# A decoder step's cache loop on one Trainium2 core: TensorE takes its slots in pairs

## The chip, the cores and the metric

The kernel runs on one core of one Trainium2 chip (trn2), in one launch. The metric is device time in microseconds. The core has five engines that run their own instruction streams and meet at semaphores: TensorE (PE in the profile, its weight loads PEld), VectorE (DVE), ScalarE (ACT), GpSimd (POOL) and SyncE (SP). Transfers between memory and the core are DMAs, issued here by SP and POOL and carried by 16 DMA engines.

## The reference

One inference step of a two-layer decoder. In each layer a prompt of 256 tokens and a group of 8 sequences with 8 new tokens each go through the same weights:

```python
h   = RMSNorm(x) @ W_in
mix = concat[ StickBreakingAttn(q,k,v) | Mamba2-SSD(z,xBC,dt) | MultiScalePool(p) ]
x   = x + mix @ W_out
x   = x + W_down( silu(causal_dwconv3(RMSNorm(x) W_gate)) * RMSNorm(x) W_up )
```

The new tokens of each sequence also attend to 2048 cached positions, that is 16 pages of 128 keys and 128 values, 8 heads of 64 each, found through a page table:

```python
z = einsum('bqhd,bkhd->bhqk', qi, k) * scale + hb
log_keep = where(mask, log_sigmoid(-z), 0.0)
later = cumsum(log_keep, axis=3, reverse=True) - log_keep
w = where(mask, exp(log_sigmoid(z) + later), 0.0)
return einsum('bhqk,bkhd->bqhd', w, v)
```

The weight of a position needs the sum over all later positions, so the pages are taken from the last to the first. All numbers are fp32.

## The kernel before

Each layer has an input projection, a mixing stage with the attention to the cache, an output projection and a gated feed-forward part. The projections take most of the time; each fp32 product there is three matmuls on split planes. The change concerns the mixing stage alone, the **cache loop**.

The loop works on two sequences at a time (a pair) and on chunks of 8 pages, 4 of each of the two sequences. `CHUNKS` is 16 for each layer: 4 pairs by 4 chunks. Every engine runs its own hand-written copy of the loop `for qn in range(CHUNKS + 3)` with 8 slots each; order within an engine is the order of the code, and a wait on a semaphore holds up all that stands behind it. What PE does:

- `key_page(q, k)` (the transposes are line 1382): page k of chunk q has landed in `kring`; four 128x128 transposes put it into PSUM bank 4 (even k) or 5 (odd k). Before that PE waits until the page two earlier has been copied out of that bank: ACT copies the even pages, DVE the odd ones (`key_copy`, lines 941 and 2033) into `kT`.
- `chunk_z(q, bb)` (1394): scores of the four pages of one sequence, four matmuls with 32 columns of the array each. `chunk_z(q, 0)` comes in slot 5 of chunk q, `chunk_z(q, 1)` in slot 1 of the next.
- From the scores ACT and DVE make the weights of the chunk: `chunk_logs` on ACT in slot 2, `chunk_relu` and `chunk_argument` (a scan) on DVE in slots 3 and 5, `chunk_weights` (the exponential, 955) on ACT in slot 6, behind the copy of key page 6.
- `weights_T(q)` (1408): four transposes of the weights at the end of chunk q + 1; ACT copies them into `wz` (`weights_out`, 965).
- `value_page(q, k)` (1426): in chunk q + 2, products of those weights with the values in `vring`, with 32 columns of the array each (in the profile eight matmuls, as every fp32 matmul here has two). The first page of a chunk waits for `wz`.
- `step(s)`: the state-space and pooling work of the layer, cut into small steps by the table `MIX`, one in a slot up to slot 101 (of 152): transposes of states (T, 1528), products with 64 rows (N, 1544), with 16 columns (Y, 1534), in 64 columns of the array (y, 1482) and others. They use PSUM banks 3 and 7 in turn; each is read by DVE or ACT in the same slot of their loops, and PE's a step waits until the step two earlier has been read.

In slot k of chunk qn PE thus runs `key_page(qn, k)`, `value_page(qn - 2, k)`, in some slots a piece of the scores, and then `step`. Chunks 0 and 1 have keys alone, chunks 2 to 15 keys and values, chunks 16 and 17 values alone. In this text a chunk is counted by qn, from its first key page on.

SP issues the loads of key pages into a ring of 8, each when PE has transposed the page 8 before it, with the loads of states between them. POOL issues the loads of value pages (`value_in`), one chunk ahead of their use and each when PE has used the page 8 before it; it also has state work of its own in the slots. After the loop come the first products of the output projection (`out_step`).

Of the kernel before, what the change touches and what calls it, by code (L numbers as in the profile page):

```python
# [79 lines left out]
CHUNKS = 4 * PAIRS  # L80
# [47 lines left out]
def build(nc, a, o):  # L128

    with ExitStack() as ctx:  # L130
# [1003 lines left out]
        def _(pe):  # L1134
            def products(l, base, n, planes, half=8, between=None, ready=None, side=None, swap=0,
# [38 lines left out]
                if n > 1:  # L1174
                    with pe.Fori(1 if between else 0, n) as i:
                        one(i + base)

            DOWN = [down for _, down in B_PART]
            def norm_sum(n):

# [51 lines left out]
            for l in range(DEPTH):  # L1232
# [136 lines left out]
                def new_keys():  # L1369
                    pe.wait_ge(n_w, l + 1)  # L1370
                    for pi in range(PAIRS):
                        mm = pe.transpose(ps[6][0:SAMP, P * pi:P * pi + P], zn[:, SAMP * pi:SAMP * pi + SAMP], ident)
                    mm.then_inc(n_T, 1)

                def key_page(q, k):

                    n = 8 * q + k
                    pe.wait_ge(k_loaded[k], l * (16 * CHUNKS) + 16 * (q + 1))
                    if n >= 2:
                        pe.wait_ge(kT_out[("act", "dve")[n % 2]], l * (CHUNKS * 4) + n // 2)  # L1380
                    for j in range(SBT):
                        mm = pe.transpose(ps[4 + n % 2][:, j * P:(j + 1) * P], kring[:, k, j * P:(j + 1) * P], ident)  # L1382
                    mm.then_inc(k_T, 1)
# [184 lines left out]
                    mm.then_inc(unit_done, 1)  # L1568

                for qn in range(CHUNKS + 3):  # L1570
                    for slot in range(8):
                        if qn < CHUNKS:
                            key_page(qn, slot)
                        if 2 <= qn < CHUNKS + 2:
                            value_page(qn - 2, slot)
                        if slot == 1 and 1 <= qn <= CHUNKS:
                            chunk_z(qn - 1, 1)
                        if slot == 1 and qn == 0:
                            new_scores()
                        if slot == 7 and qn == 0:  # L1580
                            new_keys()
                        if slot == 3 and qn >= 6 and qn % 4 == 2:
                            pair_fold((qn - 6) // 4)
                        if slot == 5 and qn < CHUNKS:
                            chunk_z(qn, 0)
                        step(8 * qn + slot)
                    if qn == CHUNKS:
                        out_step(0, 0)
                    if 1 <= qn <= CHUNKS:
                        weights_T(qn - 1)  # L1590
                    if qn == CHUNKS:
                        out_step(0, 1)
                    if qn == CHUNKS + 1:
                        out_step(1, 0)
# [53 lines left out]
        def _(dve):  # L1648
# [206 lines left out]
            for l in range(DEPTH):  # L1855
# [172 lines left out]
                def key_copy(q, k):  # L2028

                    dve.wait_ge(k_T, l * (CHUNKS * 8) + (8 * q + k + 1))  # L2030
                    if q and k % 4 == 1:
                        dve.wait_ge(q_mm, l * GROUPS + (2 * q + k // 4 - 1))
                    dve.tensor_copy(kT[k // 4][:, :, P * (k % 4):P * (k % 4) + P],
                                    ps[5][:].rearrange("p (j s) -> p j s", j=SBT)).then_inc(kT_out["dve"], 1)
# [172 lines left out]
                for qn in range(CHUNKS + 3):  # L2207
                    for k in range(8):
                        slot = 8 * qn + k
                        for s, at_ in enumerate(((CHUNKS, 1), (CHUNKS, 6), (CHUNKS + 2, 7))):  # L2210
                            if (qn, k) == at_:
                                out_lo(s)
                        if qn < CHUNKS and k % 2:
                            key_copy(qn, k)
                        if slot == 0:
                            prompt_low()
                        if slot == 1:
                            new_arguments()
                        if slot == 4:
                            new_sums()  # L2220
                        if slot == 5:
                            dve.memset(wz[:], 0.0)
                            dve.drain().then_inc(wz_zero, 1)
                        if slot == SLOT["y", 0, 0]:
                            dve.wait_ge(kv_stored, l * 64 + 64)
                        if k == 3 and 1 <= qn <= CHUNKS:
                            chunk_relu(qn - 1)
                        if k == 5 and 1 <= qn <= CHUNKS:
                            chunk_argument(qn - 1)
                        if k == 6 and qn >= 6 and qn % 4 == 2:  # L2230
                            pair_low((qn - 6) // 4)
                        if k == 7 and qn >= 5 and qn % 4 == 1:
                            pair_mask((qn - 5) // 4)
                        if slot - 3 in MIX and MIX[slot - 3][0] == "c":
                            head_weights(*MIX[slot - 3][1:])
                        step(slot)
                        norm_y(slot)
# [182 lines left out]
```

## Time and profile before

| | us |
|---|---|
| median of 3 runs | 3304.39 |
| lowest and highest | 3302.07, 3304.97 |
| span of the profiled execution | 3305.7 |
| cache loop of layer 0, first key page to last value page | about 321 to 606 |
| cache loop of layer 1 | about 1945 to 2232 |

The profile is one execution on the core. In a row of a stretch the busy times are those of PE, PEld, DVE, ACT and POOL, each with its instructions behind it. Busy time of an engine is the union of its instructions; matmuls are pipelined and their ends are modelled, so the distance between starts says more than the busy share. "Idle before" is time in which the engine had nothing running, with what released it. The chain of waits is followed back from the last instruction: at each step to what released it. The granted clock of PE is a share of 2.4 GHz; 0.5 is 1.2 GHz.

### The profile page before, as it was taken

Reading aid. Unit: us, or ns where it says so; the run is one execution under the profiler, and the core shown is the slowest. Engines: PE = TensorE matmul, PEld = TensorE weight load, DVE = VectorE, ACT = ScalarE, POOL = GpSimd, SP = SyncE. Lnnn points to the kernel's source line nnn. Section 1 sums busy time; section 2 is a strip of 40 time slices with the busy share of each in tenths; the row PEclk is TensorE's granted clock in tenths of the full one; section 3 lists DMA queues with packets and bytes.
Section 4 is the critical chain, followed back from the end, with each engine's and each line's share of the span. In section 5 each row is a group of like instructions: output and inputs, shape, how many; then the busy total and the mean of one; then the engine's idle time right before and its main releaser. Section 6 shows DMA issues by size and latency. Waiting matters only on the chain.

```text
span 3305.7 us, 62396 instructions
## 1 busy us (share of the span) xinstructions
PE 3213.3 (97%) x23776; PEld 3026.9 (92%) x23776; DVE 1898.2 (57%) x3339; ACT 1346.9 (41%) x1663; POOL 409.6 (12%) x513
## 2 busy tenths in 40 slices
PE   7999998999999999999999999989999999999998
PEld 7999665899999999999999976659999999999998
DVE  4574655466653665466746656454666546654664
ACT  4553665444433333233335546563444333333332
POOL 0000654220000000000200035531100000000002
PEclk9999999999999999999999999989999999999999
DMA  6433799744444444444544448985444444444443
GB/s 188 141 124 104 242 311 300 216 144 153 152 142 153 151 144 152 145 154 138 157 141 128 129 140 273 314 275 164 147 153 148 146 153 148 145 154 143 149 149 101
DMA packets 469101, 554.42 MB, mean 168 GB/s; under 512 B 20635, under 2 KB 414444, under 8 KB 468788
## 3 DMA queue, kind: packets, MB, share of 16 engines
q1 hardware_dynamic: 440275, 466.93, 44.3%
q0 software_dynamic: 26192, 84.73, 7.9%
q8 instruction: 117, 1.92, 0.2%
q10 hardware_dynamic: 2449, 0.27, 0.1%
q14 instruction: 68, 0.56, 0.1%
HBM read 535.50 MB, written 16.38 MB: 167 GB/s over the span
## 4 chain that ended last, share of the span: by engine, by line
PE 92%; ACT 2%; DVE 1%; issue 1%; DMA 1%; PEld 1%; ACTq 0%; DVEq 0%; PEldq 0%; POOLq 0%; POOL 0%; SPq 0%
PE ps L1157 26%; PE ps L1159 26%; PE ps L1158 26%; PE ps L1382 3%; PE ps L1426 2%; PE ps L1394 1%; PE ps L1544 1%; PE ps L1534 1%; PE ps L1471 1%; PE ps L1528 1%; DMA raw<-in_w_out 0%; PE ps L1408 0%; DMA vring<-in_cache_v 0%; ACT wz L965 0%; ACT kT L941 0%
## 5 line engine op out<-in xcount | busy, mean ns | idle before, releaser
L1654 DVE TENSOR_TENSOR wl<-raw,wh 128x1024 fp32r<-128x1024 f32 (+1 forms) x736 | 904.3, 1238 | 994.4 <-ACT wh L776 986.6
L776 ACT ACTIVATE wh<-raw 128x1024 fp32r<-128x1024 f32 (+1 forms) x736 | 764.8, 1041 | 1603.6 <-PE ps L1159 1592.7
L1157 PE MATMUL ps<-fh,wh 128*128 128x320 f32 x2816 | 870.6, 309 | 0.0
L1159 PE MATMUL ps<-fh,wl 128*128 128x320 f32 x2816 | 870.1, 309 | 0.0
L1158 PE MATMUL ps<-fl,wh 128*128 128x320 f32 x2816 | 870.1, 309 | 0.0
L1157 PEld LDWEIGHTS ps<-fh,wh 128*128 128x128 f32 x2816 | 528.5, 188 | 0.2
L1158 PEld LDWEIGHTS ps<-fl,wh 128*128 128x128 f32 x2816 | 528.5, 188 | 0.2
L1159 PEld LDWEIGHTS ps<-fh,wl 128*128 128x128 f32 x2816 | 528.5, 188 | 0.0
L1157 PE MATMUL ps<-hh,wh 128*128 128x320 f32 x1376 | 428.4, 311 | 5.6 <-DVE wl L1654 4.6
L1157 PE MATMUL ps<-ah,wh 128*128 128x320 f32 x1376 | 427.2, 310 | 0.0
L1159 PE MATMUL ps<-hh,wl 128*128 128x320 f32 x1376 | 426.1, 310 | 0.0
L1159 PE MATMUL ps<-ah,wl 128*128 128x320 f32 x1376 | 425.2, 309 | 0.0
L1158 PE MATMUL ps<-hl,wh 128*128 128x320 f32 x1328 | 411.3, 310 | 0.0
L1158 PE MATMUL ps<-al,wh 128*128 128x320 f32 x1328 | 410.3, 309 | 0.0
L1157 PEld LDWEIGHTS ps<-hh,wh 128*128 128x128 f32 x1376 | 259.2, 188 | 7.7 <-issue 5.1
L1157 PEld LDWEIGHTS ps<-ah,wh 128*128 128x128 f32 x1376 | 258.3, 188 | 1.7 <-issue 0.3
L1159 PEld LDWEIGHTS ps<-hh,wl 128*128 128x128 f32 x1376 | 259.1, 188 | 0.0
L1159 PEld LDWEIGHTS ps<-ah,wl 128*128 128x128 f32 x1376 | 258.3, 188 | 0.0
L1158 PEld LDWEIGHTS ps<-hl,wh 128*128 128x128 f32 x1328 | 250.2, 188 | 0.0
L1158 PEld LDWEIGHTS ps<-al,wh 128*128 128x128 f32 x1328 | 249.3, 188 | 0.0
L752 POOL DMA_DIRECT2D out_new_ffn_conv_prompt<-ftail x6 | 3.1, 523 | 1612.1 <-DVE ftail L1746 1612.1
L1382 PE MATMUL ps<-con,kring 128*128 128x128 f32 x1024 | 168.7, 289 | 7.6 <-ACT kT L941 6.9
(405 smaller groups left out, 3683.1 us busy)
## 6 DMA issues: line engine op xcount, KB each, us to landing
raw<-in_w_gate SPq DMA_DIRECT2D x88, 1024.0 KB, 5.1
raw<-in_w_up SPq DMA_DIRECT2D x88, 1024.0 KB, 5.0
raw<-in_w_in SPq DMA_DIRECT2D x72, 1024.0 KB, 5.2
kring<-in_cache_k SPq DMA_DIRECT2D x256, 256.0 KB, 4.2
vring<-in_cache_v POOLq DMA_DIRECT2D x256, 256.0 KB, 4.6
raw<-in_w_down SPq DMA_DIRECT2D x64, 1024.0 KB, 5.4
raw<-in_w_out SPq DMA_DIRECT2D x32, 1024.0 KB, 6.5
raw<-in_w_down SPq DMA_DIRECT2D x32, 768.0 KB, 4.6
```

Of the source, the lines that this page charges most:

```text
L776: act.activation(wh[:, s % 2, half, :], raw[:, s, half, :], ACT.Copy).then_inc(hi_done, 1)
L1157: pe.matmul(out, wh[:, s % 2, kk, w], hi(row), start=first, stop=False)
L1158: pe.matmul(out, wh[:, s % 2, kk, w], lo(row), start=False, stop=False)
L1159: mm = pe.matmul(out, wl[:, s % 2, kk, w], hi(row), start=False, stop=last)
L1382: mm = pe.transpose(ps[4 + n % 2][:, j * P:(j + 1) * P], kring[:, k, j * P:(j + 1) * P], ident)
L1394: mm = pe.matmul(ps[q % 2][32 * j:32 * j + 32, :], qp[:, q // 4, bb, j, :], kT[bb][:, j, :], start=(bb == 0), stop=(bb == 1))
L1426: mm = pe.matmul(ps[6][32 * j:32 * j + 32, 0:P], wz[:, k // 4, k % 4, j, :], vring[:, k, j * P:(j + 1) * P], start=False, stop=last)
L1471: mm = pe.matmul(bank[:, i * T:(i + 1) * T], tk[0:T, 1, h:h + 1].broadcast_to([T, P]), le, start=True, stop=True)
L1528: mm = pe.transpose(bank[:, j * P:(j + 1) * P], s_seq[i % 4][:, 4 * h + j, :], ident)
L1534: mm = pe.matmul(bank[:, j * 16:(j + 1) * 16].rearrange("p (e t) -> p e t", e=2), sT[:, i % 2, j * P:(j + 1) * P], csS[:, 2 * j:2 * j + 2, ...
L1544: mm = pe.matmul(bank[:, j * NS:(j + 1) * NS], xw[0:SAMP, (4 * h + j) * P:(4 * h + j + 1) * P], bm[:, i % 2, h * NS:(h + 1) * NS], start=T ...
L1654: dve.tensor_tensor(wl[:, s % 2, half, :], raw[:, s, half, :], wh[:, s % 2, half, :].bitcast(F32), ALU.subtract).then_inc(lo_done, 1)
```

## The change

On PE two slots are taken together: key pages k and k + 1, the step of slot k, value pages k and k + 1, the pieces of the scores and the like that stood in either slot, and the step of slot k + 1. On DVE the copy of the odd key page moves from its own slot to the head of the even slot before it. Nothing else is touched; the work is the same.

```diff
--- before.py
+++ after.py
@@ -1568,22 +1568,25 @@
                     mm.then_inc(unit_done, 1)
 
                 for qn in range(CHUNKS + 3):
-                    for slot in range(8):
+                    for slot in range(0, 8, 2):
                         if qn < CHUNKS:
                             key_page(qn, slot)
+                            key_page(qn, slot + 1)
+                        step(8 * qn + slot)
                         if 2 <= qn < CHUNKS + 2:
                             value_page(qn - 2, slot)
-                        if slot == 1 and 1 <= qn <= CHUNKS:
+                            value_page(qn - 2, slot + 1)
+                        if slot == 0 and 1 <= qn <= CHUNKS:
                             chunk_z(qn - 1, 1)
-                        if slot == 1 and qn == 0:
+                        if slot == 0 and qn == 0:
                             new_scores()
-                        if slot == 7 and qn == 0:
+                        if slot == 6 and qn == 0:
                             new_keys()
-                        if slot == 3 and qn >= 6 and qn % 4 == 2:
+                        if slot == 2 and qn >= 6 and qn % 4 == 2:
                             pair_fold((qn - 6) // 4)
-                        if slot == 5 and qn < CHUNKS:
+                        if slot == 4 and qn < CHUNKS:
                             chunk_z(qn, 0)
-                        step(8 * qn + slot)
+                        step(8 * qn + slot + 1)
                     if qn == CHUNKS:
                         out_step(0, 0)
                     if 1 <= qn <= CHUNKS:
@@ -2210,8 +2213,8 @@
                         for s, at_ in enumerate(((CHUNKS, 1), (CHUNKS, 6), (CHUNKS + 2, 7))):
                             if (qn, k) == at_:
                                 out_lo(s)
-                        if qn < CHUNKS and k % 2:
-                            key_copy(qn, k)
+                        if qn < CHUNKS and k % 2 == 0:
+                            key_copy(qn, k + 1)
                         if slot == 0:
                             prompt_low()
                         if slot == 1:
```

## Rows read from the trace of the kernel before

**Rows 1.** The page, part 1: busy us, share of the span, instructions.

```profile
PE 3213.3 (97%) x23776; PEld 3026.9 (92%) x23776; DVE 1898.2 (57%) x3339; ACT 1346.9 (41%) x1663; POOL 409.6 (12%) x513
```

**Rows 2.** Stretches, layer 0: us, busy by engine, clock, DMA share, GB/s.

```profile
420.00:480.00 60.00, 57.06 (x616) 39.83 (x617) 29.89 (x58) 35.57 (x72) 29.28 (x41) 1.00 0.96 315
...
540.00:595.00 55.00, 42.74 (x474) 24.14 (x475) 32.25 (x49) 38.90 (x61) 17.93 (x33) 0.91 0.89 291
```

**Rows 3.** PE timeline, chunk 7: start, us, line, operation, count, idle before.

```profile
441.11 0.60 PE L1382 MATMUL ps<-con,kring 128*128 128x128 f32 x4
442.02 0.43 PE L1426 MATMUL ps<-vring,wz 128*32 128x128 f32 x8 [0.31 <-ACT wz L965]
...
444.55 0.66 PE L1528 MATMUL ps<-con,s_seq 128*128 128x128 f32 x4
445.05 0.60 PE L1382 MATMUL ps<-con,kring 128*128 128x128 f32 x4
445.57 0.43 PE L1426 MATMUL ps<-vring,wz 128*32 128x128 f32 x8
445.93 0.66 PE L1382 MATMUL ps<-con,kring 128*128 128x128 f32 x4
446.52 0.43 PE L1426 MATMUL ps<-vring,wz 128*32 128x128 f32 x8
```

**Rows 4.** The same timeline, chunk 16: two value pages in a row.

```profile
588.36 0.65 PE L1426 MATMUL ps<-vring,wz 128*32 128x128 f32 x16 [0.75 <-ACT wz L965]
```

**Rows 5.** Timeline of PE's weight loads at the place of rows 3.

```profile
444.94 0.47 PEld L1382 LDWEIGHTS ps<-con,kring 128*128 128x128 f32 x4
```

**Rows 6.** Waits of PE, chunks 2 to 12, layer 0: us, times, longest.

```profile
PE ps L1426 <- ACT wz L965: 3.1, 8, 0.9
PE ps L1408 <- ACT wq L955: 3.0, 3, 1.3
PE ps L1471 <- DVE pool_lo L2133: 1.0, 1, 1.0
PE ps L1423 <- ACT wz L965: 0.7, 2, 0.4
```

**Rows 7.** The same for layer 1.

```profile
PE ps L1426 <- ACT wz L965: 2.2, 7, 0.4
PE ps L1471 <- DVE pool_lo L2133: 1.9, 1, 1.9
PE ps L1408 <- ACT wq L955: 1.2, 3, 0.4
```

**Rows 8.** Timeline of ACT at the end of chunk 6.

```profile
438.02 0.60 ACT L941 ACTIVATE kT<-ps 128x512 f32<-128x512 f32 x1 [1.85 <-PE ps L1382]
...
439.93 0.63 ACT L955 ACTIVATE wq<-wq 128x512 f32<-128x512 f32 x1
```

**Rows 9.** Chain of waits, layer 0, chunk 15: start, us, what.

```profile
574.78 0.42 PE ps L1426 x8
575.20 0.97 PE ps L1382 x4
576.17 0.59 PE ps L1426 x8
```

**Rows 10.** Stretches as in rows 2: the 10 us that moved most.

```profile
460.00:470.00 10.00, 10.00 (x112) 7.11 (x105) 4.62 (x8) 6.92 (x12) 6.03 (x8) 1.00 1.05 374
```

**Rows 11.** The same, chunks 7 and 12, layers 0 and 1 of each.

```profile
441.10:457.30 16.20, 14.56 (x162) 9.90 (x161) 7.47 (x13) 8.35 (x13) 7.84 (x11) 1.00 0.92 288
2061.40:2081.20 19.80, 19.07 (x163) 12.50 (x162) 7.65 (x13) 8.35 (x13) 7.67 (x11) 0.74 0.93 291
527.10:544.50 17.40, 15.76 (x167) 11.04 (x165) 9.84 (x17) 8.51 (x13) 8.84 (x13) 1.00 0.84 283
2150.90:2173.40 22.50, 21.78 (x166) 14.79 (x165) 10.15 (x17) 8.46 (x13) 8.79 (x12) 0.70 0.78 238
```

## The prediction

> **What bounds the kernel now.** I read the page first. TensorE (PE) is busy for 97% of the span [rows 1], so time is won where PE runs, provided PE is what the stage waits for. The change touches only the cache loop, twice some 300 us out of 3305.7. So I cut that loop into stretches: in the middle of it PE is busy for 57.06 of 60 us, at a granted clock of 1.00, VectorE (DVE) and ScalarE (ACT) for a half and somewhat more; towards the end PE falls to 42.74 of 55 [rows 2]. The middle hangs on PE, the end on something else.
>
> Busy is not work, though, so next I read PE's timeline for the distance from one start to the next. A key page is four full-array transposes, a value page eight matmuls that each use 32 columns of the array. From [rows 3]: four transposes (here T, a state step) that come after 32-column work and before full-array work take 0.50 us to the next start (444.55 to 445.05). A key page between full-array work and a value page takes 0.52 (445.05 to 445.57). A key page between two value pages takes 0.59 (445.93 to 446.52). So coming in from the narrow shape costs 0.07 and going out to it 0.09, and a key page with full-array work on both sides is 0.59 - 0.07 - 0.09 = 0.43. A value page between key pages takes 0.36 (445.57 to 445.93); two value pages in a row last 0.65 against 0.43 for one [rows 4, 3], so a value page followed by another takes 0.22. Going back to the wide shape thus costs 0.36 - 0.22 = 0.14 there and 0.07 in the page that follows. Of the stretch K V K V, 1.90 us, a part is nothing but changes of shape. That is the first thing that the change can move.
>
> The second is in the waits. At each chunk's first value page PE stands idle for the weights that ACT has to copy out after W (0.31 at 442.02 [rows 3]); over chunks 2 to 12 that is 3.1 + 0.7 us in layer 0 and 2.2 + 0.7 in layer 1, 19 waits [rows 6, 7] (the row of line 1423 reads the same in both layers and stands once). W itself, the weights' transpose, waits for ACT's exponential 3 times in each layer, 3.0 and 1.2 us. The only other wait in these stretches is one step's for DVE, 1.0 and 1.9; there is none for a load [rows 6, 7].
>
> **The change part by part.**
>
> *Fewer changes of shape.* No instruction is added or taken away. Two slots K V S, K V S become K K S, V V S. Without steps, K V K V is 2 x (0.59 + 0.36) = 1.90; K K V V is 0.50 + 0.52 + 0.22 + 0.36 = 1.60. Gain 0.30. With a full-array step S in the first slot: before, K 0.52, V 0.36, S 0.50, K 0.52, V 0.36 = 2.26; after, K 0.43, K 0.43, S 0.52, V 0.22, V 0.36 = 1.96 (S taken as four transposes). Again 0.30. A step of another shape (64 rows or 64 columns) has a change on both sides in either order, so two changes of five still go. Key and value pages meet in chunks 2 to 15; steps end at slot 101, in chunk 12. For chunks 2 to 12, where PE is the bound, that is 11 chunks x 4 pairs x 2 layers = 88 pairs: **26.4 us**. Chunks 0 and 1 have no value pages, 16 and 17 no keys and no steps, so nothing changes shape less often there: zero.
>
> *The wait for the weights.* After W, before: one key page, then the value page. After: two key pages and a step first, at least 0.43 us more. The missing time is 0.91 - 0.52 = 0.39 (441.11 to 442.02 against a page that does not wait [rows 3]). It is covered even where there is no step. The idle time of 3.8 + 2.9 = 6.7 us does not count the 0.07 by which an unhindered value page starts before the key page's modelled end (445.05 + 0.60 against 445.57), 19 times 1.3: **8.0 us**. The cover is the second key page; if that waits itself (for DVE's copy), at most these 8 us stay.
>
> *The end of the loop, chunks 13 to 15.* There the chain of waits goes value page 0.42, key page 0.97, value page 0.59, scores [rows 9], partly at half clock, and then through ACT. With the key page moved under the wait for the weights the stretch becomes two value pages, 0.65 [rows 4]: 0.42 + 0.97 + 0.59 - 0.65 = 1.3 saved at best; at full clock, 0.36 + 0.59 + 0.22 - 0.44 = 0.7, less 0.1 for the two key pages after W. Two chunks in each layer show this, and in one of them the loads that GpSimd (POOL) issues may come last: 0 to 5 us, taken **3**.
>
> *What is given back.* W needs ACT's exponential, which follows the copy of key page 6: from the copy's start to the exponential's end 439.93 + 0.63 - 438.02 = 2.54 us [rows 8]. The exponential hangs on PE's page 6, and the pair 6/7 is now 0.30 shorter. Where W waits already (6 chunks, [rows 6, 7]) the 0.30 of that pair is lost, 1.8; in all 22 chunks it would be 6.6. I take **-3**, since most chunks have no such wait.
>
> *Moved work costed at nothing.* DVE copies the odd key page before the step of the even slot, no longer after it: half of DVE's time is free there [rows 2], and the copy is wanted only when the key page two later comes. If it delayed the even steps, PE would wait up to a copy, some 0.6 us (what ACT's takes [rows 8]), less the second slot. SP issues the odd key load a little sooner. POOL waits for "value page used": the even one comes a key page and a step later, the odd one about when it did; value pages are loaded a whole chunk ahead, and in the middle PE never waits for one [rows 6, 7]. What is queued behind POOL's wait is its state work, which has several slots to spare. Nothing to either side of the loop changes; it starts earlier.
>
> Sum: 26.4 + 8.0 + 3 - 3 = 34.4. The profiled span of 3305.7 stands 1.3 above the median of 3304.4; I subtract from the median and give 1 us for steps whose inputs now are late, as two are already (1.0 and 1.9 [rows 6, 7]): **3271 us**, -1.0%. Own range 3259 to 3283: low if the two half-clock stretches of layer 1 go too (below, 8.7) and the end gives its 5; high if all the weights' wait stays and W loses everywhere (8 + 3.6).
>
> The page "TensorE: Matmul & The Clock Gate" of the Trainium skill, Part 3, speaks against this: loading weights overlaps running matmuls only when the row group differs; key pages all use every row. The trace disagrees: key page weights begin loading at 444.94 [rows 5] while T, on all 128 rows, runs from 444.55 for 0.66 [rows 3]. By that rule the sum would be the 3295 of the second rival, by the rows it is 3271.
>
> **The rivals.**
>
> *Transfers pace the middle.* The 16 DMA engines are busy at a share of 0.96 at 315 GB/s there [rows 2]; the same pages in less time need some 9% more (a chunk of some 17 us loses 4 x 0.30 + 8.0/22 = 1.56). If nothing more passes in the busier two thirds, 14 of the 22 chunks, then 14/22 of 31.4 = 20 are lost: 3291. The same time comes out if ACT's chain sets every chunk's length. Against it: one stretch of 10 us moved 374 GB/s at 1.05 [rows 10], and PE has no wait for a page in chunks 2 to 12 [rows 6, 7]. Chance 0.17, for 3283 to 3298.
>
> *The full array doesn't overlap.* If two key pages side by side cost as much as two apart, the 26.4 are gone: 3304.4 - 8 - 3 + 2 = 3295. [Rows 3 and 5] are against it: 0.04. The rule of the Trainium skill above would give this.
>
> *Slower, by the clock.* In layer 1 chunk 7 took 19.80 against 16.20 in layer 0 at the same work, chunk 12 22.50 against 17.40, at a mean granted clock of 0.74 and 0.70 [rows 11]: stretches at 1.2 GHz instead of 2.4, costing 3.6 and 5.1. Longer runs of transposes and more pressed waits at W could bring such stretches into other chunks, at 4.35 each. From eight more on (8 x 4.35 = 35) the gain is gone; in 12 more of the 22 chunks, 3271 + 52 = 3323. For it: two of 22 have it already. Against it: PE has less idle time than before, and layer 0 has none in these two. Slower by over 0.2%: 0.05; five to nine more, and so no change that shows: 0.07.
>
> **How the numbers follow.** Forecast 0.67 (3259 to 3283), transfers 0.17, no overlap 0.04, clock 0.07 and 0.05. What a measurement can tell from no change is about 0.2%, 6.6 us. Faster by more than that (under 3297.8): 0.67 + 0.17 + 0.03 = 0.87; same 0.08; slower 0.05. For 8 in 10 the range takes the forecast's own and most of the transfers': 3258 to 3292.
>
> **What would show it.** Right: PE's timeline has value pages in sixteens of some 0.65 us and key pages in eights; a key page after a key page starts 0.50 or less behind it; no idle time of PE before a value page put down to ACT's weights; waits of W for ACT grown from 4.2 us to 6 to 10; each layer's loop shorter by some 17 us, all other stages as long as before. Wrong: waits of PE for key or value loads and a DMA share above 1 in the middle (transfers); key pages 0.59 apart (no overlap); chunks at a mean clock near 0.7 in both layers (clock); or waits at the steps, where a step that comes sooner finds DVE or ACT not done.

## The result, and the profile after

The changed kernel takes **3274.01 us** (median; 3269.99 to 3287.52), the kernel before 3303.23 (3297.14 to 3304.97) beside it. The ratio is 0.9932, with a 95% interval of 0.9912 to 0.9953: 22 us faster by the ratio, 29 by the medians. The forecast was 3271 in a range of 3258 to 3292, a gain of 33 us. The time lies in the range, the direction and the mechanism are as forecast, and about a third of the gain is missing by the ratio (4 of the 33 us by the medians). Most of what follows is about that third.

The page of the changed kernel, first line and part 1, to set beside [rows 1]. The profiled execution is the slowest of the changed kernel's, some 13 us above their median, so its losses are a little larger than usual:

```profile
span 3285.7 us, 62396 instructions
...
PE 3180.7 (97%) x23776; PEld 3038.2 (92%) x23776; DVE 1912.0 (58%) x3339; ACT 1346.4 (41%) x1663; POOL 410.4 (12%) x513
```

PE does the same 23776 matmuls in 32.6 us less busy time; the span is only 20.0 us shorter. The time at half clock is 97.5 us in both executions, so it does not explain the difference: PE's own work shrank by about what was forecast, and waiting grew. The stretches tell where. First those of the kernel before that were not shown (start and end in us, length, busy time and instructions of PE, PEld, DVE, ACT and POOL, granted clock, DMA share, GB/s): chunks 2 to 12 of layers 0 and 1, chunks 13 to 15 of both, and chunk 8 of layer 0.

```profile
357.60:544.50 186.90, 179.00 (x1899) 124.23 (x1897) 103.26 (x190) 111.67 (x201) 103.53 (x137) 0.99 0.89 293
1976.80:2173.40 196.60, 190.51 (x1897) 131.75 (x1896) 104.36 (x189) 111.80 (x201) 105.88 (x140) 0.93 0.86 281
544.50:588.40 43.90, 33.55 (x364) 17.93 (x365) 25.55 (x40) 29.93 (x51) 13.34 (x25) 0.92 0.89 289
2173.40:2215.60 42.20, 32.76 (x360) 18.15 (x358) 25.54 (x40) 30.02 (x51) 13.44 (x25) 0.92 0.88 289
457.30:473.10 15.80, 15.49 (x166) 10.96 (x165) 6.95 (x11) 9.92 (x16) 8.82 (x12) 1.00 1.06 373
```

The same stretches of the changed kernel, then chunk 8 of layers 0 and 1, and chunks 7 and 12 of layer 0 for [rows 11]:

```profile
357.50:542.60 185.10, 173.23 (x1898) 132.41 (x1897) 111.93 (x191) 111.78 (x201) 104.18 (x136) 0.95 0.89 297
1971.00:2157.20 186.20, 175.47 (x1899) 134.05 (x1898) 109.55 (x189) 111.71 (x201) 106.93 (x141) 0.94 0.89 295
542.60:583.80 41.20, 29.55 (x360) 19.47 (x358) 25.66 (x40) 29.66 (x50) 13.22 (x25) 0.92 0.91 302
2157.20:2198.50 41.30, 29.52 (x360) 19.46 (x357) 25.66 (x40) 29.79 (x50) 13.43 (x25) 0.92 0.90 302
452.60:473.90 21.30, 17.81 (x166) 13.59 (x165) 7.02 (x11) 10.14 (x16) 7.51 (x11) 0.84 0.97 321
2065.10:2088.10 23.00, 19.18 (x166) 14.80 (x165) 7.05 (x11) 10.14 (x16) 7.55 (x11) 0.78 0.90 294
437.60:452.60 15.00, 13.38 (x162) 10.26 (x161) 7.47 (x13) 8.35 (x13) 7.61 (x11) 1.00 0.95 301
523.40:542.60 19.20, 17.58 (x166) 13.39 (x164) 9.90 (x17) 8.49 (x13) 9.12 (x13) 0.82 0.85 300
```

Chunk 7 is what the forecast had in mind: 15.00 us for 16.20 at the same work and full clock. Chunk 8 is the opposite: 21.30 and 23.00 for 15.80. Chunks 2 to 12 together gain 1.8 + 10.4 = 12.2 us where 26.4 + 8 - 3 - 1 = 30.4 were forecast. An average gain of 1.43 in chunk 8 would have brought it to 14.4, so chunk 8 alone loses 6.9 + 8.6 = 15.5 of the missing 18.2. The remaining 2.7 are the difference of larger parts. Chunks 2 to 4 of both layers gain 3.3 us where six times 1.43 = 8.6 were forecast. Chunk 12 of both layers and chunk 7 of layer 1 gain 6.1 where 4.3 were forecast, since half-clock stretches stand there in one execution and not in the other: [rows 11] has them in chunks 7 and 12 of layer 1, the changed kernel in chunk 12 of both layers. The end of the loop, chunks 13 to 15, gains 2.7 + 0.9 = 3.6 for the 3 forecast. The other 4.2 of the 20.0 lie outside these stretches, where nothing was forecast; they are less than the 7.8 us between the lowest and the highest time of the kernel before.

PE's timeline of chunk 8 in layer 0, the analogue of [rows 3], shows both the gain and the loss:

```profile
452.15 0.66 PE L1408 MATMUL ps<-con,wq 128*128 128x128 f32 x4 [1.62 <-ACT wq L955]
452.65 1.04 PE L1382 MATMUL ps<-con,kring 128*128 128x128 f32 x8
453.61 0.64 PE L1426 MATMUL ps<-vring,wz 128*32 128x128 f32 x16
454.07 1.04 PE L1394 MATMUL ps<-kT,qp 128*32 128x512 f32 x8
...
456.94 0.64 PE L1426 MATMUL ps<-vring,wz 128*32 128x128 f32 x16
457.52 0.66 PE L1528 MATMUL ps<-con,s_seq 128*128 128x128 f32 x4
461.31 0.66 PE L1382 MATMUL ps<-con,kring 128*128 128x128 f32 x4 [3.13 <-DMA kring<-in_cache_k]
462.32 0.66 PE L1382 MATMUL ps<-con,kring 128*128 128x128 f32 x4 [0.36 <-DMA kring<-in_cache_k]
462.82 3.14 PE L1534 MATMUL ps<-csS,sT 128*128 128x16 f32 x16
```

Two key pages with a value page behind them take 453.61 - 452.65 = 0.96 from the first start to that of the value page. With 0.52 for the page ahead of the value page [rows 3], the first of the two costs 0.44; 0.43 was forecast for a key page with full-array work on both sides. Two value pages take 0.46 to the next narrow work (453.61 to 454.07) and 0.58 to the next wide work (456.94 to 457.52), as 0.22 + 0.36 says. There is no idle time ahead of the value page at 453.61, where chunk 7 before had a wait of 0.31 for the weights [rows 3]. In exchange W waits 1.62 for the exponential, and then, at 458.18, PE stands still for 3.13 us for a key page. After that the clock row of the trace falls to 0.5 for 6.8 us (from 463.1), and the sixteen matmuls of Y take 3.14.

PE's waits in chunks 2 to 12 of layer 0, to set beside [rows 6] (us in total, times, longest):

```profile
PE ps L1408 <- ACT wq L955: 3.8, 4, 1.6
PE ps L1382 <- DMA kring<-in_cache_k: 3.5, 2, 3.1
PE ps L1471 <- DVE pool_lo L2136: 2.1, 1, 2.1
PE ps L1426 <- ACT wz L965: 0.8, 1, 0.8
```

and of layer 1, beside [rows 7]:

```profile
PE ps L1408 <- ACT wq L955: 4.0, 5, 1.6
PE ps L1382 <- DMA kring<-in_cache_k: 3.8, 2, 3.4
```

The value pages' wait is gone (the 0.8 is the first value page of chunk 13, at 544.44), W waits 7.8 us where it waited 4.2, and a row that before had none heads the new ones: key pages that wait for their load.

At the end of the loop the chain of waits of layer 0 in chunk 15, [rows 9] before, now reads (start, us, what):

```profile
578.74 0.49 ACT kT L941
...
579.38 1.06 PE ps L1382 x8
580.44 0.62 PE ps L1426 x16
...
583.47 5.44 DMA vring<-in_cache_v
```

The value page between the two key pages is out of the chain, as worked out; the copies of keys on ACT stand in it, and a load that POOL issues comes last of all, as was held possible.

### The profile page after: what moved, and what is told of

It is laid out like the page before. It is cut to its first block, busy times and chain, and to the rows that moved or that the text cites. A ratio compares the mean times of both kernels' runs of the same rounds, so it can differ in the third digit from the quotient of the medians.

```text
span 3285.7 us, 62396 instructions
## 1 busy us (share of the span) xinstructions
PE 3180.7 (97%) x23776; PEld 3038.2 (92%) x23776; DVE 1912.0 (58%) x3339; ACT 1346.4 (41%) x1663; POOL 410.4 (12%) x513
## 3 DMA queue, kind: packets, MB, share of 16 engines
q1 hardware_dynamic: 440275, 466.93, 44.3%
## 4 chain that ended last, share of the span: by engine, by line
PE 90%; DVE 2%; ACT 2%; DMA 2%; issue 1%; PEld 1%; DVEq 0%; ACTq 0%; SPq 0%; PEldq 0%; POOLq 0%; POOL 0%
PE ps L1157 26%; PE ps L1159 26%; PE ps L1158 26%; PE ps L1382 3%; PE ps L1394 1%; PE ps L1426 1%; PE ps L1544 1%; PE ps L1534 1%; DMA kring<-in_cache_k 1%; DMA vring<-in_cache_v 1%; PE ps L1471 1%; DMA raw<-in_w_out 0%; PE ps L1408 0%; ACT kT L941 0%; ACT L955 0%
## 5 line engine op out<-in xcount | busy, mean ns | idle before, releaser
L604 POOL DMA_DIRECT2D vring<-in_cache_v x256 | 139.4, 545 | 237.8 <-issue 131.4
```

Source lines behind the costliest of these rows:

```text
L604: pool.dma_start(vring[:, k, :], a["cache_v"][l, page].rearrange("s h d -> s (h d)")).then_inc(v_loaded[k], 16)
```

## The experiments

All ratios are to the kernel before, run beside the kernel in question on the same chip, with 95% intervals. The length of a chunk is the distance between its first key page and the next chunk's in the profiled execution. "The change" is the changed kernel above.

### The change once more

The changed kernel without any edit, to see what of the above returns.

> The changed kernel unchanged, beside the variants on one chip. Theory 1 (two late key pages in chunk 8 give back part of the gain): the times scatter between 3268 and 3288 us, and a profile shows PE waiting for key loads in chunk 8, 2 to 4 us in a layer, with a half-clock stretch behind it. Theory 2 (transfers pace the whole middle): 3274 us, with waits for loads in several chunks. Theory 3 (the clock alone): half-clock stretches without a wait ahead of them.

Measured: 3277.27 us (3271.86 to 3291.24), ratio 0.9937 (0.9915 to 0.9959). The profile is of an execution at the median, span 3274.8 us. Chunk 8 takes 21.8 and 20.0 us, and key pages wait for their loads again, 5.0 us in 4 places (7.3 us in 4 places of the whole run above). That is what the first theory expected.

So the loss in chunk 8 belongs to the kernel and not to one execution. Chunk 12, at half clock in both layers above, is so only in layer 0 here (19.3 us); in layer 1 it takes 16.1. That stretch comes and goes, and no step of the argument should rest on it.

### One part alone: fewer changes of shape

K V V K S S instead of K K S V V S: the value pages are in pairs, so that there are fewer changes of shape, but no second key page and no step stands between W and the first value page.

```diff
                         if qn < CHUNKS:
                             key_page(qn, slot)
-                            key_page(qn, slot + 1)
-                        step(8 * qn + slot)
                         if 2 <= qn < CHUNKS + 2:
                             value_page(qn - 2, slot)
                             value_page(qn - 2, slot + 1)
...
+                        if qn < CHUNKS:
+                            key_page(qn, slot + 1)
+                        step(8 * qn + slot)
                         step(8 * qn + slot + 1)
```

> Fewer changes of shape without the cover for the weights: per two slots PE runs key page, value page, value page, key page, step, step. Two changes of shape in each pair as in the changed kernel, but the first value page of a chunk stands one key page behind the weights' transpose, as before. Theory 1 (26 us from the shape, 8 from the cover): 3280 to 3286 us, the idle time before value pages put down to ACT's weights is back at 5 to 7 us. Rival (the cover brings most): 3292 to 3298 us.

Measured: 3283.72 us (3279.7 to 3286.53), ratio 0.9950 (0.9932 to 0.9968), 16.5 us. In the chunks that nothing else disturbs the gain is what four pairs at 0.30 should give, and a little less: chunks 8, 9, 10 and 11 of layer 0 take 14.7, 16.6, 17.2 and 17.1 us for 15.8, 17.6, 18.1 and 18.3, that is 1.1, 1.0, 0.9 and 1.2 for 1.2. Chunks 5 and 7 gain 0.7 and 0.8; chunk 6 gains nothing, as its wait for the weights grows from 0.31 to 0.92 and a step waits 0.41. Over chunks 2 to 12 of both layers the wait for the weights is 10.3 us, where 5 to 7 were expected and 6.7 stood before. Chunk 4 pays: 20.9 us for 18.4 in layer 0, at full clock, and 22.6 for 17.9 in layer 1. There two steps stand side by side, and the second finds its input not done. PE's timeline of chunk 4:

```profile
391.99 1.16 PE L1503 MATMUL ps<-xtok,xw 128*128 128x128 f32 x8
394.87 0.45 PE L1482 MATMUL ps<-seg,xtok 128*64 128x128 f32 x4 [1.72 <-ACT cs L1012]
```

The price of a change of shape is confirmed where PE has nothing to wait for. The 26.4 us of the sum lie above the interval (10.6 to 22.4): the steps' inputs set the pace in chunk 4, and the weights come later in relation to a faster PE.

### The other part alone: a cover for the weights' wait

From the kernel before: K S V in each slot. The changes of shape are as many as before (where the step is full-array work), but a step stands between W and the first value page, in the chunks that have a step in slot 0 (chunk 8 has none).

```diff
                         if qn < CHUNKS:
                             key_page(qn, slot)
+                        step(8 * qn + slot)
                         if 2 <= qn < CHUNKS + 2:
                             value_page(qn - 2, slot)
...
-                        step(8 * qn + slot)
```

> The cover alone: as before one slot at a time, but the step runs between the key page and the value page (key page, step, value page), so four changes of shape in two slots as before, while the first value page of a chunk now has a step and not only a key page between it and the weights' transpose. Theory 1: 5 to 9 us faster than before, 3292 to 3297; the idle time before value pages put down to ACT's weights falls from some 11 to under 4 us. Rival (the order of steps against pages is what helps, not the shape): 15 us or more faster.

Measured: 3290.68 us (3283.22 to 3298.3), ratio 0.9983 (0.9971 to 0.9996), 5.6 us. The wait of value pages for weights falls from 10.0 us in 21 places of the whole run to

```profile
PE ps L1426 <- ACT wz L965: 5.2, 8, 1.2
```

of which 0.6 lie in chunks 2 to 12, in chunk 8 of the two layers (5.3 before [rows 6, 7]). Chunks 5, 9, 10 and 11 take 14.8, 17.0, 17.6 and 17.6 us for 15.2, 17.6, 18.1 and 18.3: 0.4 to 0.7 each, which is the 0.39 of the prediction and a little more. The 8 us of the sum lie inside the interval's 1.3 to 9.6 us. Shape alone and cover alone add up to 22 us, the change to 21 to 22. That the two agree is a coincidence and does not show that the parts simply add: shape alone loses in chunk 4, where the change does not, and the change loses in chunk 8, where neither part alone waits for a load (14.7 us there with shape alone, 15.7 and, partly at half clock, 17.3 with the cover).

### The copy on VectorE back in its own slot

The order of PE is the change's; DVE copies the odd key page in its own slot again.

```diff
-                        if qn < CHUNKS and k % 2 == 0:
-                            key_copy(qn, k + 1)
+                        if qn < CHUNKS and k % 2:
+                            key_copy(qn, k)
```

> The changed order on PE, but DVE copies the odd key page in its own slot, behind the even slot's step, as before. Theory 1 (the move on DVE costs and brings little): within 4 us of the changed kernel, 3271 to 3281. Rival (the early copy delays the even steps in chunks 4 and 13, where nothing was won): 4 us or more faster, chunk 13 back to 15 us. The other side (the early copy is needed, as the next odd key page waits for it): slower, with waits of PE for DVE's copies.

Measured: 3277.48 us (3268.5 to 3287.97), ratio 0.9942 (0.9920 to 0.9965), no different from the change. PE now waits for DVE's copies, 13.3 us in the whole run instead of 1.9:

```profile
PE ps L1382 <- DVE kT L2036: 13.3, 12, 2.4
```

The waits for key loads in chunk 8 are there as in the change, 5.4 us. Chunk 13 falls from 15.8 to 15.3 us in both layers, chunks 0 and 3 of layer 1 rise by 1.2 (partly at half clock) and 0.6. So the moved copy is worth its place in some chunks and costs in others, and on balance nothing that can be measured. The place where it costs is read in the change's trace, ACT and DVE in chunk 13: DVE takes the copy at 546.17 ahead of the product that ACT waits for, ACT's copy of a key page stands behind that wait, and PE behind the copies.

```profile
546.17 0.69 DVE L2036 COPY kT<-ps 128x512 f32<-128x512 f32 x1
546.78 1.00 DVE L2191 SCALAR_TENSOR_TENSOR y<-y,par,rstd 128x320 f32<-128x320 f32 x2
...
547.36 0.47 ACT L1029 ACTIVATE y_hi<-y 128x320 fp32r<-128x320 f32 x1 [2.48 <-DVE y L2191]
547.73 0.58 ACT L941 ACTIVATE kT<-ps 128x512 f32<-128x512 f32 x1
```

### The loads of three states spread out

Ahead of chunk 8, in slot 59 (chunk 7), SP issues the loads of three states, 512 KB each, one right after the other, and only then the next key loads. Here they are issued in slots 59, 61 and 63, on the change and, for comparison, on the kernel before.

```diff
-                        if slot == SLOT["y", 2, 3] + 3:
-                            for i in range(1, 4):
+                        for i in range(1, 4):
+                            if slot == SLOT["y", 2, 3] + 1 + 2 * i:
                                 state_in(i)
```

> The changed kernel, but SP issues the loads of states 1, 2 and 3 two key pages apart (slots 59, 61, 63) instead of all three in slot 59, ahead of key page 4 of chunk 8. Theory 1: no wait of PE for key pages in chunk 8, the chunk takes 15 to 16 us in both layers (21.3 and 23.0 before), the median falls by some 6 to 12 us to 3262 to 3268 and scatters less. Theory 2: the wait moves to other chunks and the time stays within 3 us of the changed kernel's. Theory 3: the half-clock stretch in chunk 8 stays although the wait is gone, and 3 to 5 us of the loss with it.

> The kernel before with the same spreading of the state loads and nothing else. Theory 1: PE did not wait for key pages there, so no change: within 4 us of 3303. Theory 2 (the loads cost the kernel before as much): 6 us or more faster.

Measured, on the change: 3271.18 us (3268.96 to 3277.74), ratio 0.9915 (0.9894 to 0.9937): slower than the 3262 to 3268 of the first theory, and not clear of the change's 0.9932. On the kernel before: 3296.78 (3290.78 to 3301.95), ratio 0.9986 (0.9973 to 1.0), 4.6 us or little more than nothing. On the change chunk 8 falls to 14.2 and 14.3 us. But a wait for loads now stands in chunk 9, 2.4 and 1.8 us, and that chunk takes 20.1 and 18.0 us for the 15.9 of an undisturbed one. What holds it is SP's queue in chunk 8, ahead of the key loads for chunk 9 (the queue's own waits, 455 to 475 us):

```profile
SPq L480 <- DMA out_new_ssm_sample<-s_seq: 4.0, 1, 4.0
```

The load of the next state waits until the state before it in its buffer has been stored, and the key loads stand behind that wait.

### The later states' loads later as well

In addition, the loads of states 4 to 7 are issued three slots later, when the store is done. The second expectation is for the same kernel, run once more.

```diff
                         for i in range(4, NB):
-                            if slot == SLOT["N", i - 4, 1] + 3:
+                            if slot == SLOT["N", i - 4, 1] + 6:
                                 state_in(i)
```

> The changed kernel with the loads of states 1 to 3 two key pages apart and the loads of states 4 to 7 issued three slots later (by then the store that each must wait for has landed, so SP holds no key load behind that wait). Theory 1: the waits for key pages in chunk 9 (1.9 and 2.4 us) go too, chunk 9 takes 16 us, 3262 to 3268 us. Theory 2 (transfers pace the middle): waits for key or value pages turn up in another chunk, 3270 or more.

> The changed kernel with both loads of states moved, once more and unchanged, beside the variant below. Theory 1: no wait of PE for key pages, 0.8% to 0.9% faster than before.

Measured: 3268.94 us (3260.66 to 3274.24), ratio 0.9913 (0.9893 to 0.9933); and 3263.77 (3255.48 to 3267.8), ratio 0.9882 (0.9861 to 0.9903). It is the fastest kernel here, below both the kernel before and the change. The mean of the two ratios, 0.990, is 34 us: the 33 of the forecast. PE has no wait for a key page in the whole run. Stretches of this kernel (the first profile): chunks 2 to 12 of both layers, and chunk 8 of both.

```profile
357.80:532.70 174.90, 166.51 (x1899) 128.22 (x1898) 113.28 (x192) 111.61 (x201) 104.02 (x136) 0.99 0.92 312
453.00:467.20 14.20, 14.20 (x167) 11.35 (x166) 8.60 (x11) 9.93 (x16) 7.50 (x11) 1.00 1.07 368
1960.80:2137.20 176.40, 168.85 (x1897) 129.62 (x1896) 112.41 (x189) 111.42 (x201) 106.63 (x140) 0.98 0.92 311
2054.40:2068.50 14.10, 14.10 (x166) 11.25 (x165) 8.55 (x11) 9.93 (x16) 7.40 (x11) 1.00 1.07 368
```

In chunk 8 PE is busy for all of 14.20 us, at a DMA share of 1.07 and 368 GB/s: with the loads in this order the transfers keep up with the faster loop. There is little to spare. From its landing to the moment at which PE asks for it, the key page with the least slack has 1.1 us, in chunk 9. Chunks 2 to 12 gain 12.0 + 20.2 = 32.2 us for the 30.4 of the sum. That match is in part luck: 8.7 of them are the two half-clock stretches of [rows 11] that this execution does not have, and it has one of its own in chunk 12 of layer 1 (19.3 us for 16.1). Without these the gain is 32.2 - 8.7 + 3.2 = 26.7. PE's timeline in the middle of chunk 8, beside that of the change:

```profile
458.38 1.04 PE L1382 MATMUL ps<-con,kring 128*128 128x128 f32 x8
459.26 1.86 PE L1534 MATMUL ps<-csS,sT 128*128 128x16 f32 x16
```

Key pages 4 and 5 follow without a gap, and the same sixteen matmuls of Y take 1.86 for 3.14. In the three profiles of kernels that wait for loads in chunk 8 (the change twice, and the one with the copy back in its slot) there is a half-clock stretch in that chunk in both layers; in the three whose loads are spread there is none. So there the stretch came with the wait and went with it.

What these runs leave open: the same loads moved in the kernel before were tried in part only (the ratio 0.9986 above), so of the 34 us up to some 5 may belong to the loads by themselves and not to the pairs. The trace of that part speaks against it: chunks 5 to 12 are as long in both layers as in layer 0 before, to 0.1 us, and that execution is 11 us shorter with 76.5 us at half clock for 97.5. The later loads of states 4 to 7 were not tried on the kernel before.

### Value pages in fours

If two value pages in a row save 0.30 a pair, four in a row save once more. With the later loads of the last kernel, K K S V V V V S at the first and the last pair of a chunk and no value pages between:

```diff
-                        if 2 <= qn < CHUNKS + 2:
-                            value_page(qn - 2, slot)
-                            value_page(qn - 2, slot + 1)
...
+                    def values(k):
                         if 2 <= qn < CHUNKS + 2:
+                            for n in range(4):
+                                value_page(qn - 2, k + n)
+
+                    keys(0)
+                    step(8 * qn)
+                    values(0)
...
+                    keys(6)
+                    step(8 * qn + 6)
+                    values(4)
```

> The loads as in the run before, and value pages in fours: two groups in a chunk where the changed kernel has four, the second just before the last step. If a change of shape costs 0.15 us (0.30 for a pair of changes), 44 pairs of changes fewer are 13 us: 3250 to 3258, as long as the weights' transpose does not wait more. Rival (ACT's chain now sets the chunks): waits at the weights' transpose or for ACT's copies grow by as much, 3262 to 3270.

Measured: 3286.24 us (3278.35 to 3295.02), ratio 0.9965 (0.9950 to 0.9979): slower than with pairs, and slower than both theories had it. The saving is there where nothing waits: chunk 7 takes 13.2 us, for 15.0 in pairs and 16.2 before. Of the 1.8 us against pairs 1.3 are W's wait for the exponential (0.35 for 1.62) and some 0.5 the shape. But PE waits for the copies of keys in the whole run

```profile
PE ps L1382 <- ACT kT L941: 30.3, 23, 4.7
```

where it waited 11.3 us in the change. Most of that lies in chunks 13 to 15, which take 42.0 and 44.3 us in the two layers for 41.5 and 41.4 in pairs. In the middle chunk 5 goes from 13.7 to 18.3 us (a wait of 1.64 for such a copy, then a granted clock of 0.81 over the chunk), chunk 8 from 14.2 to 17.7 and 18.9, with waits for states, for value pages and for a copy on ACT, and at a clock of 0.90 and 0.82.

Then one group of four only, pages 2 and 3 taken with 0 and 1, the rest in pairs:

```diff
-                        if 2 <= qn < CHUNKS + 2:
-                            value_page(qn - 2, slot)
-                            value_page(qn - 2, slot + 1)
+                        if 2 <= qn < CHUNKS + 2 and slot != 2:
+                            for n in range(4 if slot == 0 else 2):
+                                value_page(qn - 2, slot + n)
```

> As late_again, but the value pages 2 and 3 of a chunk stand with 0 and 1, so the pair of slots 2 and 3 changes no shape for values; the second half stays in pairs. If a pair of changes costs 0.25 to 0.30 us wherever PE is the bound: 22 pairs fewer, 5 to 7 us faster than late_again. Rival (ACT's chain has no room left): the waits of PE for ACT's copies or at the weights' transpose grow by as much, within 3 us of late_again or slower.

Measured: 3273.35 us (3270.77 to 3274.11), ratio 0.9919 (0.9900 to 0.9937), behind the 0.9882 of the pairs run beside it. Chunks 7 to 11 of layer 0 gain 0.1 to 0.3 each, as one change of shape less would; chunks 3 and 4 lose more, since the value pages are wanted a slot or two before they land (5.4 us of waits for such loads in chunks 3, 4 and 6, where pairs have none), and ACT's copies are late more often (15.5 us of waits in the run, 11.4 with pairs). Of the three sizes tried, two is the best here.

## Why the prediction was right, and where it was not

**Changes of shape, 26.4 us: right in size where PE is the bound, too much for the whole loop.** By the starts, a second key page costs 0.44 us where 0.43 was read off. Chunks 5 to 12 of layer 0 without a disturbance went from 15.2, 16.8, 16.2, 15.8, 17.6, 18.1, 18.3 and 17.4 to 13.7, 15.5, 15.0, 14.2, 15.9, 16.7, 16.7 and 16.1 us (chunks 8 and 12 from the kernel with later loads): 1.45 each on average. The sum had (26.4 + 8 - 3) / 22 = 1.43. But it took PE as the bound in all of chunks 2 to 12, and in chunks 3 and 4 it is not (see the steps below); alone, the shape was worth 16.5 us (10.6 to 22.4).

**The overlap of weight loads: right, and that rival is out.** Key pages side by side stand 0.44 us apart, not 0.59. The Trainium skill, "TensorE: Matmul & The Clock Gate", Part 3, has the overlap only where the row group differs; the trace disagrees, since all key pages use all rows. Part 2 of the same page adds a second case, weights that go to a background buffer, in which the rows do not matter; the trace fits that case, though nothing in it shows the buffer itself.

**The weights' wait, 8 us: right.** It is gone from chunks 2 to 12; by itself, with a step as the cover, it was worth 5.6 (1.3 to 9.6), part of which may be the clock (below).

**What W gives back, 3 us: right in kind, and in size partly by the clock.** Its wait in these chunks went from 4.2 to 7.8, so 3.6; 6 to 10 was named as the sign. But the 4.2 is low because chunks 7 and 12 of layer 1 ran partly at half clock before [rows 11]: W waited 0.41 behind each, where it waited 1.33 in layer 0. In layer 0 alone the growth is 3.8 - 3.0 = 0.8, so 1.6 for two layers. Where W waits longest, the wait went from 1.33 to 1.62, by the 0.30 of one pair.

**The end of the loop, 3 us: right in sum.** 2.7 + 0.9 = 3.6 in chunks 13 to 15, made of a chunk 13 that is 0.9 and 0.5 us longer (0.5 of it DVE's moved copy ahead of work that ACT waits for, as the run with the copy back in its slot shows) and of chunks 14 and 15 that are shorter by more. "Costed at nothing" was wrong for the copy in that one place. (The low end of the prediction's own range, 3259, is 3260 by its terms: 3271 - 8.7 - 2.)

**Steps, 1 us: mis-sized.** Chunk 4 does not gain: 18.4 and 17.9 us before, 18.3 and 18.3 after, so 2 x 1.43 + 0.3 = 3.2 are lost. Its steps wait for DVE, ACT and POOL (0.3 to 0.7 us each), and a PE that comes sooner only waits longer. Chunk 3 of layer 0 does not gain either (16.6 to 16.7): the step at its end waits 2.1 us for DVE where it waited 1.0. In the kernel with later loads, whose chunks 3 and 4 run at full clock in both layers, the two together take 35.0 and 34.3 us for 35.0 in layer 0 before, so some 5 us are lost there against four times 1.43. The waits of one such step stood in the trace of before, 1.0 and 1.9; that whole chunks could hang on them was not drawn from that.

**The loads, costed at nothing: this is the step that failed.** The prediction read that PE has no wait for a load in chunks 2 to 12, and took that for room. No wait only says that the slack is not negative. In the trace of before SP issues three loads of states at 447.88, the key loads behind them from 454.13 on; the load of key page 4 of chunk 8 lands about 461.9, and PE asks for it 1.7 us later. In the change the same load lands at about 461.3, and PE asks at 458.18. The load came when it always had; PE had come 5.5 us earlier. (In layer 1 the slack was 5.5 us before, as PE was held back by the half-clock stretch in chunk 7, and it was used up as well.) SP's queue in the change (start, us, what):

```profile
443.75 6.28 SPq L480 DMA_DIRECT2D s_seq<-in_state_ssm  x3
450.79 7.26 SPq L493 DMA_DIRECT2D kring<-in_cache_k  x5
```

PE transposes key page 4 of chunk 7 from 444.27, and with that the place of the ring comes free; the load for chunk 8 goes out at 450.79, behind the states, and then needs 10.5 us. In the trace of before the place was free at 448.68, the load went out at 454.13 and needed 7.8 us: a delay of the same kind, 13.3 us in all for 17.0, which the slack still covered. The landing times, first of the loads issued in the 13.6 us before the states, then of those in the 14.4 us from the states on (KB each, median us to landing):

```profile
vring<-in_cache_v POOLq DMA_DIRECT2D x9, 256.0 KB, 4.4
kring<-in_cache_k SPq DMA_DIRECT2D x8, 256.0 KB, 4.4
...
vring<-in_cache_v POOLq DMA_DIRECT2D x8, 256.0 KB, 6.6
kring<-in_cache_k SPq DMA_DIRECT2D x6, 256.0 KB, 9.1
s_seq<-in_state_ssm SPq DMA_DIRECT2D x3, 512.0 KB, 12.0
```

So the delay is in two parts, some 5.5 us of waiting to be issued and some 6 us of slower landing. The Trainium skill, "DMA: Bandwidth & Descriptors", "Two DMAs through the same engine are not ordered", says that in one queue of one DMA engine descriptors start in order but are pipelined. The trace fits that, as the small loads behind three of 512 KB took 9.1 us for 4.4; but the value loads on POOL's queue slowed too, 6.6 for 4.4, so not all of it is the order in one queue. The experiments hold the rest: spreading the three loads takes the wait out of chunk 8 and leaves one at the next place where SP's queue stands (a store), and with that place cleared as well the waits are gone and the gain comes near the forecast one. The losses in chunk 8 were 15.5 us in the first profile and, by the same count, 13.0 in the second (21.8 and 20.0 for 2 x 14.4). By the ratios of the kernel with later loads against the change, 0.990 against 0.993, it is 12 us with an uncertainty of some 7.

**The rival "transfers pace the middle", 0.17: right in one chunk, not in two thirds of them.** It had the rate as the limit in 14 of 22 chunks, and waits for loads at a DMA share above 1 as its sign. Both signs are there, in chunk 8 of each layer. From the issue of the late key load to its landing (layers 0 and 1 of the change, stretches as above):

```profile
450.79:461.26 10.47, 6.02 (x72) 4.41 (x72) 2.29 (x4) 7.60 (x13) 4.70 (x8) 1.00 1.05 367
2063.39:2073.98 10.59, 6.02 (x72) 4.41 (x72) 2.19 (x4) 7.63 (x13) 5.29 (x9) 1.00 1.06 371
```

So the DMA engines were as full while PE waited as in the kernel with later loads, where it never waits (1.07, 368 GB/s); the 0.97 and 0.90 of the whole chunk take in the work behind the wait. With the engines full, it is the order of the loads that decided whether the key page came in time. In the other chunks from 2 to 12 no load is waited for, and over all of them the last kernel runs at a share of 0.92: the rate does not pace the whole middle.

**The clock: a part, but not the rival.** The granted clock is at a half for 97.5 us of the profiled execution before and for 97.5 after, so no more of it than before. But its place moved: 6.8 and 10.2 us of it stand behind the wait in chunk 8, and 6.8 at half clock cost 3.4. Of the 7.1 us that chunk 8 of layer 0 takes beyond 14.2, 3.5 are the wait and the rest is about that. What decides where such a stretch falls stays open: chunk 12 has one in some executions and none in others, in the change and in the kernel before.

The clock also has a share in the measured gains. Half clock costs half its length, so 0.001 of the mean granted clock is some 3.3 us, an estimate from the spans. The means over the runs, with those of the kernel before beside them, are 0.9881 for 0.9887 (the change once more), 0.9904 for 0.9887 (shape alone), 0.9906 for 0.9896 (cover alone), 0.9903 for 0.9896 and 0.9912 for 0.9886 (later loads). By that, about 5.6 of the 16.5 us of shape alone, 3.3 of the 5.6 of the cover and 5 of the 34 with later loads are less time at half clock. Whether that comes from the edits or from chance is not shown. What is left of the 34 is some 29. That 34 meets the forecast's 33 is luck to this extent: the clock's share about makes up for what the steps lost beyond the 1 us allowed for them.

## What to carry to other kernels

Before a loop is made faster, look not only for waits on loads but for the slack of each load, from its landing to the moment at which it is asked for; the least slack, not the average, says how much faster the loop may become (here one chunk of 11 in each layer, with 1.7 us of slack in layer 0, ate a third of the gain). Where bulk loads and small loads share a queue, place the bulk ones one at a time between the small ones, and keep waits for stores out of it. Group work of one shape on the array in twos where each change of shape costs some 0.15 us, and stop where the other engines' copies start to come late. Before one execution is compared with another, compare their time at half clock.

## What the runs showed of the hardware that was not expected

- A wait of PE of 3.1 us for a load was followed by 6.8 us (10.2 in layer 1) at a granted clock of 0.5, 1.2 GHz, so that the price of the wait doubled; with the wait gone the same work ran at full clock. It is not a rule: a wait of 1.8 us in chunk 9 (loads of three states spread out, layer 1) had no such stretch behind it, and in the cover alone chunk 8 of layer 0 has one of 3.4 us without a wait for a load.
- Stretches at half clock of 6.8 to 13.7 us also fall where PE has no wait for a load, as in chunks 7 and 12 of layer 1 before [rows 11], and they move between layers and executions of one kernel: chunk 12 takes 16.1 or 19.3 us in the change, 17.4 or 22.5 before.
- Three loads of 512 KB ahead of loads of 256 KB on one queue doubled the landing time of the latter, 4.4 to 9.1 us, while loads of the same size on the other queue went from 4.4 to 6.6 us. The DMA engines were full (a share of 1.05 at 367 GB/s). In another order, as full as before (1.07, 368 GB/s), no key page came late.
